# Hierarchical MoE routing: ranks of the experts within their groups instead of two rounds of first-maximum selection

## The reference

```python
grp_prob = softmax((hf @ w_rg) + b_rg, axis=-1)              # [512, 4]
p_grp, g_idx = lax.top_k(grp_prob, 1)                        # the best group, first one on a tie
exp_logits = ((hf @ w_re) + b_re).reshape(-1, 4, 4)
sel_logits = take_along_axis(exp_logits, g_idx[:, :, None], axis=1)[:, 0]
w_top, e_loc = lax.top_k(softmax(sel_logits, axis=-1), 2)    # its two best experts, first one on a tie
w_top = p_grp * w_top / sum(w_top)
e_glob = g_idx * 4 + e_loc
# y[token] = sum over the two experts of gate * down(silu(gate_proj(x)) * up_proj(x))
```

## Time and profile before

| | before |
|---|---|
| time, median of 3 runs | 794.58 us (792.91 to 797.77) |
| span of the profiled execution | 791.7 us |
| PE busy | 747.9 us, 94% of the span |
| DVE busy | 603.7 us, 76% |
| ACT busy | 461.6 us, 58% |
| POOL busy | 78.0 us, 10% |
| chain that ended last | PE 72%, DVE 15%, ACT 6%, DMA 4%, issue 3% |
| mean granted TensorE clock | 0.987 |

### The profile page before, as it was taken

How to read it: one execution, slowest core, us unless ns; L and a number is a source line. 1 busy time by engine, 2 the same in 40 slices (tenths; PEclk the granted TensorE clock), 3 DMA queues, 4 the chain that set the end, 5 groups by cost and what they waited for, 6 DMA issues and landing times.

```text
span 791.7 us, 10886 instructions
## 1 busy us (share of the span) xinstructions
PE 747.9 (94%) x3680; PEld 607.8 (77%) x3680; DVE 603.7 (76%) x930; ACT 461.6 (58%) x689; POOL 78.0 (10%) x94
## 2 busy tenths in 40 slices
PE   5899999999999898889999999999999999999994
PEld 3664858788898787678787787888888888888882
DVE  5767482997799877835548568899899999999882
ACT  5952333131233988621559333787888888887782
POOL 0000000000000000000000001122222232222111
PEclk9999999999999999999999998999999999999997
DMA  8830203020120200022130675999999999999741
GB/s 291 298 107 1 84 23 106 27 80 1 38 96 27 78 31 1 2 62 97 54 116 18 246 294 182 420 364 385 379 372 383 373 391 372 369 369 383 306 159 21
DMA packets 28542, 146.53 MB, mean 185 GB/s; under 512 B 4791, under 2 KB 6711, under 8 KB 21976
## 3 DMA queue, kind: packets, MB, share of 16 engines
q1 hardware_dynamic: 23320, 135.53, 45.3%
q0 software_dynamic: 5184, 10.50, 5.0%
HBM read 141.81 MB, written 12.58 MB: 195 GB/s over the span
## 4 chain that ended last, share of the span: by engine, by line
PE 72%; DVE 15%; ACT 6%; DMA 4%; issue 3%; SPq 0%; POOL 0%; DVEq 0%; ACTq 0%; POOLq 0%
PE bank L1992 17%; PE bank L2378 11%; PE bank L2380 10%; PE bank L2379 10%; PE bank L1930 9%; PE bank L1937 3%; DMA slot<-in_w_down 2%; PE bank L2373 2%; PE bank L2004 1%; ACT w_hi L727 1%; PE bank L2292 1%; PE bank L2290 1%; PE bank L2291 1%; DVE w_lo L1165 1%; PE bank L2415 1%
## 5 line engine op out<-in xcount | busy, mean ns | idle before, releaser
L1849 DVE TENSOR_TENSOR e_lo<-slot,e_hi 128x1024 fp32r<-128x1024 f32 x192 | 221.4, 1218 | 9.4 <-ACT e_hi L1045 9.3
L1045 ACT ACTIVATE e_hi<-slot 128x1024 fp32r<-128x1024 f32 x192 | 188.2, 1061 | 7.7 <-DMA slot<-in_w_down 4.9
L1165 DVE TENSOR_TENSOR w_lo<-w_raw,w_hi 128x1024 fp32r<-128x1024 f32 x41 | 49.4, 1222 | 69.8 <-ACT w_hi L727 69.6
L727 ACT ACTIVATE w_hi<-w_raw 128x1024 fp32r<-128x1024 f32 x41 | 42.7, 1057 | 96.9 <-DMA w_raw<-in_w_in 63.2
L2378 PE MATMUL bank<-e_hi,hgT_hi 128*128 128x512 f32 x240 | 95.0, 396 | 0.3 <-DVE hgT_lo L1861 0.3
L2380 PE MATMUL bank<-e_hi,hgT_lo 128*128 128x512 f32 x240 | 93.6, 390 | 0.0
L2379 PE MATMUL bank<-e_lo,hgT_hi 128*128 128x512 f32 x240 | 93.4, 389 | 0.0
L2378 PEld LDWEIGHTS bank<-e_hi,hgT_hi 128*128 128x128 f32 x240 | 45.2, 189 | 9.5 <-DVE hgT_lo L1861 0.7
L2380 PEld LDWEIGHTS bank<-e_hi,hgT_lo 128*128 128x128 f32 x240 | 45.1, 188 | 9.6
L2379 PEld LDWEIGHTS bank<-e_lo,hgT_hi 128*128 128x128 f32 x240 | 45.1, 188 | 8.9
L2378 PE MATMUL bank<-e_hi,gaT_hi 128*128 128x512 f32 x120 | 48.1, 401 | 0.0
(11 more groups left out here) (395 smaller groups left out, 1671.6 us busy)
## 6 DMA issues: line engine op xcount, KB each, us to landing
slot<-in_w_down SPq DMA_DIRECT2D x16, 2048.0 KB, 16.6
slot<-in_w_gate SPq DMA_DIRECT2D x16, 2048.0 KB, 14.6
slot<-in_w_up SPq DMA_DIRECT2D x16, 2048.0 KB, 16.0
w_raw<-in_w_in SPq DMA_DIRECT2D x18, 512.0 KB, 3.5
w_raw<-in_w_out SPq DMA_DIRECT2D x8, 512.0 KB, 3.7
w_raw<-in_w_k_mem SPq DMA_DIRECT2D x4, 512.0 KB, 6.1
x_in<-in_x SPq DMA_DIRECT2D x4, 512.0 KB, 9.2
w_raw<-in_w_v_mem SPq DMA_DIRECT2D x4, 512.0 KB, 6.0
```

Of the source, the lines that this page charges most:

```text
L727: act.activation(w_hi[ring(m)][:], w_raw[ring(m)][:], ACT.Copy).then_inc(s_wh, 1)
L1045: act.activation(e_hi[buffer(b, j)][:], slot[slot_][:, 1024 * part:1024 * (part + 1)], ACT.Copy).then_inc(s_ehi, 1)
L1165: dve.tensor_tensor(w_lo[slot_][:], w_raw[slot_][:], w_hi[slot_][:].bitcast(F32), ALU.subtract)\
L1849: dve.tensor_tensor(e_lo[slot_][:, at_], slot[slot_][:, at_], e_hi[buffer(b, j)][:].bitcast(F32), ALU.subtract)\
```

## The change

Routing is computed by ranks. The logits of groups and experts go to separate arrays (`gl`, `el`), which takes a third DVE instruction per tile. For each group of 4 experts, every expert is compared with every other (`compare`: is_gt and is_equal over 4 x 4 pairs), equal ones count only if they stand before (`break_ties`, times the table `less`), the two are added (`all_over`) and summed to a rank (`ranks`). This is done for tiles 0 to 2 at once, between `tile_logits(2)` and `x2T_lo(3, (1,))`, and for tile 3 after its logits, interleaved with the one-hot of the group. `onehots` is then "rank below 2, times the chosen group" in one instruction, and the semaphore that PE waits for counts to 1 instead of 4. What followed (both one-hots, chosen expert, the difference for ACT) is made afterwards from rank and el. ACT, POOL and SP have the same instructions as before. PE's matmuls are the same too, the 18 keep_clock matmuls among them.

```diff
             def tile_logits(i):
...
-                free(dve.scalar_tensor_tensor(lg[:, i, :], bank(job)[:, 0:20], r, part_, ALU.mult, ALU.add), job)
+                dve.scalar_tensor_tensor(gl[:, i, :], bank(job)[:, 0:NG], r, part_[:, 0:NG], ALU.mult, ALU.add)
+                free(dve.scalar_tensor_tensor(el[:, NE * i:NE * (i + 1)], bank(job)[:, NG:NG + NE], r, part_[:, NG:NG + NE],
+                                              ALU.mult, ALU.add), job)
+            def pairs_of(lo, hi):
+                q = slice(NG * lo, NG * hi)
+                n = NG * (hi - lo)
+                other = el3[:, q].unsqueeze(2).to_broadcast([P, n, EPG, EPG])
+                own = el3[:, q].unsqueeze(3).to_broadcast([P, n, EPG, EPG])
...
+            def compare(lo, hi):
+                n, other, own, over, tied, _ = pairs_of(lo, hi)
+                dve.tensor_tensor(over, other, own, ALU.is_gt)
+                return dve.tensor_tensor(tied, other, own, ALU.is_equal)
+            def break_ties(lo, hi):
+                return dve.tensor_tensor(tied, tied, before.to_broadcast([P, n, EPG, EPG]), ALU.mult)
+            def all_over(lo, hi):
+                return dve.tensor_tensor(over, over, tied, ALU.add)
+            def ranks(lo, hi):
+                return dve.tensor_reduce(rank, over.rearrange("p q e f -> p (q e) f"), AX.X, ALU.add)
...
             tile_logits(2)
+            wait_freed(dve, ("router", TT - 2))
+            link(compare(0, TT - 1))
+            link(break_ties(0, TT - 1))
+            link(all_over(0, TT - 1))
+            ranks(0, TT - 1)
             x2T_lo(3, (1,))
             tile_xn(3)
             tile_logits(3)
             wait_freed(dve, ("router", TT - 1))
+            dve.tensor_reduce(R(80, 4), gl, AX.X, ALU.max)
+            link(compare(TT - 1, TT))
+            dve.tensor_tensor(ohg, gl, bc(R(80, 4), 4), ALU.is_equal)
+            link(break_ties(TT - 1, TT))
+            dve.tensor_tensor(scored, ohg, first4, ALU.mult)
+            link(all_over(TT - 1, TT))
+            dve.tensor_reduce(R(152, 4), scored, AX.X, ALU.max)
+            link(ranks(TT - 1, TT))
+            link(dve.tensor_tensor(ohg, scored, bc(R(152, 4), 4), ALU.is_equal))
+            dve.scalar_tensor_tensor(onehots[:].rearrange("p (q e) -> p q e", e=EPG), rank, 2.0, in_group, ALU.is_lt, ALU.mult)\
+                .then_inc(s_oh, 1)
...
-            pe.wait_ge(s_oh, TT)
+            pe.wait_ge(s_oh, 1)
```

More of the change, by code:

```diff
@@ L1660, in tile_xn @@
                     .then_inc(s_xn, 1)
-            lg = R3(0, NG + NE)
+            gl, el = R3(0, NG), R(16, TT * NE)
+            el3 = el.rearrange("p (q e) -> p q e", e=EPG)
             def tile_logits(i):
@@ L1668, in tile_logits @@
                 link(dve.scalar_tensor_tensor(part_, bank(job)[:, 20:40], r, row("b_router"), ALU.mult, ALU.add))
-                free(dve.scalar_tensor_tensor(lg[:, i, :], bank(job)[:, 0:20], r, part_, ALU.mult, ALU.add), job)
+                dve.scalar_tensor_tensor(gl[:, i, :], bank(job)[:, 0:NG], r, part_[:, 0:NG], ALU.mult, ALU.add)
+                free(dve.scalar_tensor_tensor(el[:, NE * i:NE * (i + 1)], bank(job)[:, NG:NG + NE], r, part_[:, NG:NG + NE],
+                                              ALU.mult, ALU.add), job)
+            before = less[:, 0:EPG, 0:EPG].unsqueeze(1)
+            def pairs_of(lo, hi):
[3 more added lines that the diff above has]
+                own = el3[:, q].unsqueeze(3).to_broadcast([P, n, EPG, EPG])
+                over = rt[:, 1380 + 64 * lo:1380 + 64 * hi].rearrange("p (q e f) -> p q e f", e=EPG, f=EPG)
+                tied = rt[:, 900 + 64 * lo:900 + 64 * hi].rearrange("p (q e f) -> p q e f", e=EPG, f=EPG)
+                return n, other, own, over, tied, rt[:, 440 + NE * lo:440 + NE * hi]
+            def compare(lo, hi):
[3 more added lines that the diff above has]
+            def break_ties(lo, hi):
+                n, _, _, _, tied, _ = pairs_of(lo, hi)
+                return dve.tensor_tensor(tied, tied, before.to_broadcast([P, n, EPG, EPG]), ALU.mult)
+            def all_over(lo, hi):
+                _, _, _, over, tied, _ = pairs_of(lo, hi)
+                return dve.tensor_tensor(over, over, tied, ALU.add)
+            def ranks(lo, hi):
+                _, _, _, over, _, rank = pairs_of(lo, hi)
+                return dve.tensor_reduce(rank, over.rearrange("p q e f -> p (q e) f"), AX.X, ALU.add)
             dve.wait_ge(ld["wr"], 16)
@@ L1714, in _ @@
             wait_freed(dve, ("router", TT - 1))
-            gl = lg[:, :, 0:NG]
-            link(dve.tensor_reduce(R(80, 4), gl, AX.X, ALU.max))
-            dve.tensor_tensor(R3(84, 4), gl, bc(R(80, 4), 4), ALU.subtract).then_inc(s_r1, 1)
[L1718 to L1757, removed]
@@ L1758, in _ @@
-            link(ins)
+            first4 = row("first4").unsqueeze(1).to_broadcast([P, TT, 4])
+            ohg, scored = R3(120, 4), R3(136, 4)
+            dve.tensor_reduce(R(80, 4), gl, AX.X, ALU.max)
[5 more added lines that the diff above has]
+            dve.tensor_reduce(R(152, 4), scored, AX.X, ALU.max)
@@ new lines, in _ @@
+            link(ranks(TT - 1, TT))
+            link(dve.tensor_tensor(ohg, scored, bc(R(152, 4), 4), ALU.is_equal))
+            rank = rt[:, 440:440 + TT * NE].rearrange("p (q e) -> p q e", e=EPG)
+            in_group = R(120, TT * NG).unsqueeze(2).to_broadcast([P, TT * NG, EPG])
+            dve.scalar_tensor_tensor(onehots[:].rearrange("p (q e) -> p q e", e=EPG), rank, 2.0, in_group, ALU.is_lt, ALU.mult)\
+                .then_inc(s_oh, 1)
+            both = R(300, 128).rearrange("p (g e) -> p g e", e=NE)
@@ L1759, in _ @@
+            for r in range(2):
+                ins = dve.scalar_tensor_tensor(rt[:, 300 + 64 * r:364 + 64 * r].rearrange("p (q e) -> p q e", e=EPG), rank, float(r),
+                                               in_group, ALU.is_equal, ALU.mult)
+            link(ins)
+            dve.tensor_tensor(R3(84, 4), gl, bc(R(80, 4), 4), ALU.subtract).then_inc(s_r1, 1)
             chosen = R(1830, 8)
             picked = R(1700, 128).rearrange("p (g e) -> p g e", e=NE)
-            link(dve.tensor_tensor(picked, both, row("expert").unsqueeze(1).to_broadcast([P, 2 * TT, NE]), ALU.mult))
@@ L1762, in _ @@
-            link(dve.tensor_reduce(chosen, picked, AX.X, ALU.add))
+            values = R(640, 128).rearrange("p (r n) -> p r n", r=2)
+            dve.tensor_tensor(picked, both, row("expert").unsqueeze(1).to_broadcast([P, 2 * TT, NE]), ALU.mult)
+            link(dve.tensor_tensor(values, both.rearrange("p (r t) e -> p r (t e)", r=2), el.unsqueeze(1).to_broadcast([P, 2, TT * NE]),
+                                   ALU.mult))
+            dve.tensor_reduce(chosen, picked, AX.X, ALU.add)
+            link(dve.tensor_reduce(R(176, 8), values.rearrange("p r (t e) -> p (r t) e", e=NE), AX.X, ALU.add))
@@ L1764, in above @@
+            dve.tensor_tensor(R(200, 4), R(180, 4), R(176, 4), ALU.subtract).then_inc(s_r3, 1)
             def above(dst, x, bounds, op):
```

## The result

| | before | changed |
|---|---|---|
| time, median of 22 runs | 795.76 us (792.44 to 798.84) | 797.4 us (795.63 to 799.14) |
| ratio to before | | 1.0024, 95% interval 1.0013 to 1.0035 |
| span of the profiled execution | 791.7 us | 795.8 us |
| mean granted TensorE clock | 0.987 | 0.981 |

The changed kernel is slower by 0.24%, 1.9 us (1.0 to 2.8). The forecast was 795.7 on a median of 794.58, +1.14 us.

The account below looks back on a forecast made before the run. PE work bounds the kernel; in this stretch DVE's routing and PE's 18 unread matmuls meet at 476.7. hT_lo 1.29 later moves DVE's counts from 478.00 to 479.14: 794.58 + 1.14 = 795.7 us, range 793.0 to 798.4.

Parts of the forecast that it names:

- C: Slower rival: half clock through all 18 unread matmuls, or repeated-element views costing double; 796.1 to 798.1 us, chance 0.20.
- A: Main case: PE's 18 unread matmuls and the late hT_lo set the count's start; 795.7 us, chance 0.52.
- Third logits instruction: DVE, tile 2's logits: the added 4-element instruction takes 0.15 us, so the logits end at 468.79.
- Ranks of three tiles: DVE ahead of the last hT_lo: five 192-element instructions take 1.72 us; 1.29 of the new work is on the path.
- C's second ground: DVE compares on views with a repeated innermost element cost twice per element: 0.2 us more each, 0.4 in all.
- Routing proper: DVE from the last logits to onehots: eleven instructions in 1.95 us instead of 4.88; onehots 1.49 earlier.
- the half rule: Skill's DRAIN rule as read: each DVE operation waits for an empty pipe, semaphores cost nothing extra; sum +1.31 us.
- The router half at the clock of before: PE's last router half, ahead of the 18 unread matmuls, keeps its duration, so those matmuls start just 1.29 us later.
- The 18 matmuls: PE's unread matmuls ahead of the count take 5.83 us as before, so the count starts at 478.03.
- B: Faster rival: full clock while the 18 unread matmuls run; 792.1 to 794.2 us, point 793.5, chance 0.24.
- What DVE waits for: DVE idles about 2 us before the counts, released by PE; onehots is ready about 2.9 us before the count.
- The rest only shifts: From DVE's counts to the expert loop and beyond, nothing takes the +1.14 us delay back or multiplies it.

Follow-up runs that it names:

- e1: Kernel before plus the five rank instructions (192 elements each) on DVE ahead of the last hT_lo, result unused; ratio 1.0038 (1.0023 to 1.0054).
- e7: Kernel before plus the five rank instructions put five times over ahead of the last hT_lo, unused; ratio 1.0127 (1.0098 to 1.0157).
- e5: Kernel before with 8 instead of 18 unread matmuls ahead of the count; ratio 1.0007 (0.999 to 1.0024).
- e8: Kernel before with 48 instead of 18 unread matmuls ahead of the count; ratio 1.0089 (1.006 to 1.0117).
- e3: Changed kernel with the ranks of tiles 0 to 2 moved behind the last hT_lo and xn of tile 3; ratio 1.0023 (1.0004 to 1.0042).
- e11: Changed kernel with all four tiles' ranks behind the last logits and 8 unread matmuls instead of 18, a repeat run; ratio 0.998 (0.9967 to 0.9993).
- e10: Changed kernel run again without edits; ratio to before 1.0032 (1.0018 to 1.0047).
- e4: Changed kernel with nothing done ahead, the ranks of all four tiles made behind the last logits; ratio 1.0002 (0.998 to 1.0024).

## Why the prediction was right, and where its size was off

The side (a little slower, within 1%) and the mechanism were right: DVE's new work ahead of the last hT_lo, and PE's program order behind it. The size was not: +1.14 was forecast, +1.9 measured, and 797.4 lies in the range of C (796.1 to 798.1), not at A (795.7). What happened is A's path with a part of C's half clock on it. The spread of 4.9 us in three runs also made the prediction too careful about what can be told apart: 22 runs gave the 0.24% to within 0.11.

- **Third logits instruction.** The first compare was to start 468.82 - 466.43 = 2.39 behind the add. It starts at 2.37.
- **Ranks of three tiles.** 1.72 forecast, 470.53 to 472.24 = 1.71 measured; hT_lo 1.29 later forecast, 1.26 measured; PE's idle 1.90 and 1.86. e1 and e7 show that this is the cost. The two compares, on views with a repeated element, took 0.36 and 0.35 like the 0.36 of the row before, so C's second ground did not come true.
- **Routing proper.** 1.95 forecast; 475.32 + 0.23 = 475.55 to 477.28 + 0.22 = 477.50 is 1.95. The row at 470.80 starts 0.27 behind the one at 470.53, which lasts 0.36, so neighbours without a wait overlap. The prediction held the Trainium skill against this ("VectorE: DVE Perf Modes", "The DRAIN you can't avoid"), but with half of what stands there: the section adds, "A next op that is not held starts earlier", and with that the trace agrees. That a semaphore costs nothing extra the trace does not bear out: the linked neighbour at 471.19 starts 0.39 behind 470.80. The sum by the half rule (+1.31) was nearer only by accident.
- **The router half at the clock of before.** This is the step that failed. I moved PE's 18 matmuls by 1.29, as if the 8 router matmuls ahead of them kept their 0.91. They took 1.73, since half clock began before them: +0.82. By the table (from the start of the router half, 0.75 behind hT_lo, to the unread matmuls) this was so in all five profiles with the late hT_lo; of the nine others two had it in full (e5, e8) and two in part (e3, e11: 0.3). The fall itself came no earlier with the late hT_lo (3.3 to 4.9 us behind the add in those five, 3.1 to 5.4 in the nine); the router half, from 4.8 on (12.2 in e7), came after it each time. One profile of before, where the fall was later than the router half, was no measure of that. Under C it stood as "up to 0.5 more", with a chance of 0.20 for the whole of C. It also made the logits of tile 3 wait 0.60 for PE, so that `onehots` came 0.87 earlier and not 1.49.
- **The 18 matmuls.** 5.83 forecast, 5.94 measured. Half clock lasted longer, but part of it fell on the router half. C's bigger part, all 18 at half clock (7.7), did not happen in any profile; B's full clock in them neither. In e10, the same code, they took 6.46, so which part of them falls into half clock is luck: in e10 the stage is 0.8 us longer still.
- **What DVE waits for.** The forecast was about 2 us of idle before the counts, and 2.9 between `onehots` and the count; measured 2.55 and 3.15.
- **The rest only shifts.** From DVE's counts to the expert loop 16.13 before, 16.10 now.

Sum: 1.26 + 0.82 + 0.11 = 2.19 for the count (10.31 to 12.49 is 2.18), less 0.27, for DVE was itself late for the counts before (1.26 us behind the count's start) and waits for them now (0.99): 1.91 at DVE's counts, 1.88 at the expert loop, 1.14 forecast.

## What to carry to other kernels

When two engines' chains meet nearly together, read the one that the chain of waits does not name before shortening the other: here 18 unread matmuls ended within 0.1 us of the routing and held back all that it gained. Work done "ahead" belongs behind what another engine is already waiting for: the idle ahead of hT_lo was 0.6 us and the work 1.9, and behind hT_lo or at the very end the same work cost nothing in the stage (26.6 to 27.7 us; of the three timed ratios e3's, 1.0023, does not fit). Filler that was sized to a chain has to be sized anew when the chain gets shorter.

## What the runs showed of the hardware

- TensorE fell to half clock in this stage in each of the 14 profiles, between 3.1 and 5.4 us behind the last residual add of tile 3 (by the granted clock of stretches of 1 us). PE had been on matmuls of 40 columns before, and its idle was 0.6 us in all where the ranks were not ahead of hT_lo; in e5 the clock fell 0.2 us into that idle, in e8 0.5 us into it. So the fall needed no long idle. At 0.50 a router matmul of 40 columns starts every 0.21 us instead of 0.11.
- The same instructions ahead of the stage ended at different times in each profile: with one and the same code up to it, the last residual add stands at 466.43 before, 469.35 in e5 and 469.63 in e8; over all profiles it stands from 465.89 (e10) to 470.74 (e4). e5 has a granted clock of 0.98 from 200 to 400 us, and 0.97 in the first 100, where before has 1.00 in both. That agrees with the Trainium skill, "TensorE: Matmul & The Clock Gate", Part 1, which has the watch over activity run free of the kernel. The span of one profile is therefore no measure of an effect of 2 us here; a stage from a common event is a better one, to 0.6 to 0.8 us.
- What half clock costs at one place can be made up a few us later (e5: 1.37 us lost by the counts, stage 0.1 us longer). Its price has to be read over the whole stretch up to dense work.
